# Down weights in runs of four rows, and gate and up products that take every fourth weight column

## The chip, the core and the metric

The kernel runs on one core of one Trainium2 chip. The metric is the device time of one execution, in microseconds (us); lower is better. The kernel before takes 1104.15 us, the median of 3 runs between 1103.52 and 1104.58. A core has a tensor engine (PE, with its weight loads shown apart as PEld), a vector engine (DVE), a scalar engine (ACT), a GpSimd engine (POOL), SyncE (SP), which here issues most transfers, and 16 DMA engines.

## The reference

One step of a one-layer encoder over 1104 tokens (64 sample tokens, 16 meta tokens and 1024 prompt tokens) with width 1024. A mixer comes first (projection, windowed pooling, gated linear attention, output projection, residual), then a mixture of experts: each token picks one of 4 groups and in it 2 of 8 experts, so 2 of 32. All in f32. The part that the change touches, cut to its core:

```python
D_EXPERT = D_MODEL // 2            # 512 hidden units for each expert
def expert_block(args):
    xb, e = args
    h = jax.nn.silu(xb @ w_eg[e]) * (xb @ w_eu[e])
    return h @ w_ed[e]
...
ys = lax.map(expert_block, (xs, block_e)).reshape(R, D)
ys = ys.astype(jnp.float32) * slot_gate[:, None]
out = jax.ops.segment_sum(ys, slot_tok, num_segments=T + 1)[:T]
```

`w_eg` and `w_eu` are 1024 x 512 for each expert, `w_ed` is 512 x 1024. The hidden units are summed over in the last product, so they may stand in any order, if it is the same in `h` and in the rows of `w_ed`.

## The kernel before

The tokens stand in 9 tiles of 128. A first stage, up to about 500 us, runs over the tiles: projections (`features`, L1178), attention, the output projection (L1303), the router, and the ranks of the tokens within their experts. Normalized rows go to a buffer in HBM, `hn_rows`. The copies that normalize them, L550 and L620 on ACT, read the 1024 numbers of a row in the order k, p from a layout p, k, so every eighth number is read; L555 is a copy with a scale that reads neighbouring numbers.

The expert stage runs over 32 experts, `expert(t, b)` with e = 2t + b, each with one block of 96 tokens. All is double-buffered by b. For one expert:

- GpSimd gathers 96 rows of `hn_rows`; TensorE turns them in eight pieces (`turn_rows`, L1166) and DVE writes them as `rowsT`, 128 x 8 x 96 (`xnT` or `hnT` in the trace).
- `up` (L1407 to L1414) forms the gate and then the up product. The hidden units go to the output's partitions: the weights are the operand that is loaded into the array, and the 96 token columns stream. Of the 512 units a block m takes 128, in two strips q of 64, which use the two halves of the array's columns side by side; k runs over eight parts of the width of 1024. That makes 4 x 8 x 2 = 64 products each for gate and up. The trace has two records, each with a weight load, for one such f32 product, so 256 of L1412 for an expert.
- ACT and DVE form `hid` = silu(gate) x up, 128 partitions (units) by 4 blocks of 96 tokens.
- `down` (L1423, L1429) sums over the units: `hid` is loaded as weights, and `wd[b][:, k, ...]` streams, k being the block of units.
- ACT copies the result out of PSUM and GpSimd scatters it to `pick_rows` in HBM.

The rows of the next expert are turned between `up` and `down`. The order on each engine is written out by hand, with semaphores between engines.

The weights come from HBM by SyncE's queue, 2 MB each: `load_weights(t, b)` issues gate (L394), up (L399) and down (L402). Each waits until its buffer of two experts ago is free: the gate buffer after `pe_g`, the up buffer after `pe_u2`, the down buffer after `pe_d`. In SBUF, gate and up lie as 128 partitions x 8 x 512: partition p holds eight neighbouring rows of the matrix, one run of 16 KB in HBM. Down lies as 128 x 4 x 1024: partition p holds the rows p, 128 + p, 256 + p and 384 + p, four runs of 4 KB. Unit 128m + p stands at partition p of block m, so `up` takes 64 neighbouring columns of its weights.

After the 32 experts a block for experts with over 96 tokens (L1472 on) would run; it uses the same functions and its own loads (L427 to L429). A last stage adds each token's two results and normalizes.

Of the kernel before, what the change touches and what calls it, by code (L numbers as in the profile page):

```python
# [28 lines left out]
P = 128  # L29
# [26 lines left out]
FF = D // 2  # L56
KF = FF // P
NL = GROUPS + NE
BLOCK = 96
# [58 lines left out]
def wait_parted(eng, sem, value, parted):  # L118


    eng.wait_ge(sem, value)
    if not isinstance(value, int):
        eng.sem_inc(parted, 1)
# [32 lines left out]
def build(nc, x_all, state_pool, state_gla, norm_mix, w_in, w_gate_up, b_gate, w_pool, pool_scale, gla_norm, w_out,  # L156
# [5 lines left out]
    with ExitStack() as ctx:  # L162
# [3 lines left out]
        def sem(name):  # L166
            return ctx.enter_context(nc.semaphore(name))
# [16 lines left out]
        wd = [arena[:, starts["d", b]:starts["d", b] + EW].rearrange("p (k n) -> p k n", k=KF) for b in range(2)]  # L184
# [140 lines left out]
        s = {n: sem(n) for n in names}  # L325
        g_in = [sem(f"g_in{b}") for b in range(2)]
        u_in = [sem(f"u_in{b}") for b in range(2)]
        d_in = [sem(f"d_in{b}") for b in range(2)]
# [18 lines left out]
        def _(sp):  # L347
# [44 lines left out]
            def load_weights(t, b):  # L392
                e = 2 * t + b
                sp.dma_start(wg[b], w_eg[bass.ds(e * D, D), :].rearrange("(p k) n -> p k n", k=KD)).then_inc(g_in[b], 16)  # L394
                if isinstance(t, int) and b == 1:
                    sp.wait_ge(s["pe_wout"], TILES)
                if not isinstance(t, int):
                    sp.wait_ge(s["pe_u2"], 2 * (e - 1))
                sp.dma_start(wu[b], w_eu[bass.ds(e * D, D), :].rearrange("(p k) n -> p k n", k=KD)).then_inc(u_in[b], 16)  # L399
                if not isinstance(t, int):  # L400
                    sp.wait_ge(s["pe_d"], e - 1)
                sp.dma_start(wd[b], w_ed[bass.ds(e * FF, FF), :].rearrange("(k p) n -> p k n", p=P)).then_inc(d_in[b], 16)  # L402

            sp.wait_ge(s["pe_v"], TILES)
            load_weights(0, 0)
            load_weights(0, 1)
            sp.wait_ge(s["sA_ready"], TILES)
            for p in range(PAIRS):
# [4 lines left out]
            with sp.Fori(1, NE // 2) as t:  # L413
                for b in range(2):

                    sp.wait_ge(s["pe_g"], 2 * t + b - 1)
                    load_weights(t, b)
# [5 lines left out]
            with sp.If(n_x > 0):  # L423
                with sp.Fori(0, EXTRA) as n:
                    with sp.If(n < n_x):
                        e = sp.value_load(steer[0:1, bass.ds(n + 1, 1)], min_val=0, max_val=NE - 1)
                        sp.dma_start(wg[0], w_eg[bass.ds(e * D, D), :].rearrange("(p k) n -> p k n", k=KD)).then_inc(s["x_w"], 16)  # L427
                        sp.dma_start(wu[0], w_eu[bass.ds(e * D, D), :].rearrange("(p k) n -> p k n", k=KD)).then_inc(s["x_w"], 16)
                        sp.dma_start(wd[0], w_ed[bass.ds(e * FF, FF), :].rearrange("(k p) n -> p k n", p=P)).then_inc(s["x_w"], 16)  # L429

                        wait_parted(sp, s["x_stored"], 16 * n + 16, s["parted"])
            sp.dma_start(g_fin, norm_final.partition_broadcast(P)).then_inc(s["g_fin_in"], 16)
# [729 lines left out]
        def _(pe):  # L1162
            mm = nc.tensor.matmul

            def turn(out, src, n):
                return nc.tensor.transpose(out, src, ident[0:n, 0:n])  # L1166
# [218 lines left out]
            for n in range(2):  # L1385
                for g in range(NG):
                    last = turn(bank[2 + n][0:HIST, g * P:(g + 1) * P], u_keep[:, n, g, :], P)
# [8 lines left out]
            SW = P // STRIPS  # L1396
# [10 lines left out]
            def up(out, w, b, blocks=range(KF)):  # L1407

                for n, m in enumerate(blocks):
                    for k in range(KD):  # L1410
                        for q in range(STRIPS):
                            last = mm(out[q * SW:(q + 1) * SW, n * BLOCK:(n + 1) * BLOCK], w[:, k, m * P + q * SW:m * P + (q + 1) * SW],  # L1412
                                      rowsT[b][:, k, :], start=k == 0, stop=k == KD - 1)
                return last  # L1414

# [24 lines left out]
            def expert(t, b, last=False):  # L1440
                e = 2 * t + b
                pe.wait_ge(s["eT_ready"], 2 * e + 2)
                pe.wait_ge(g_in[b], 16 * t + 16)
                up(bank[2 + b], wg[b], b).then_inc(s["pe_g"], 1)
                pe.wait_ge(u_in[b], 16 * t + 16)

                for half in range(2):
                    up(bank[4 + half], wu[b], b, HALVES[half]).then_inc(s["pe_u2"], 1)
                if not last:
                    turn_rows(e + 1, 1 - b, 16 * (t + b) + 16)  # L1450
                pe.wait_ge(d_in[b], 16 * t + 16)
                pe.wait_ge(s["hid_ready"], 2 * e + 2)
                if not (isinstance(t, int) and e == 0):
                    pe.wait_ge(s["ye_ready"], YE_STEPS * e)
                down(b).then_inc(s["pe_d"], 1)
# [21 lines left out]
            with pe.If(n_x > 0):  # L1477
                with pe.Fori(0, EXTRA) as n:
                    with pe.If(n < n_x):
                        pe.wait_ge(s["x_rows"], 16 * n + 16)  # L1480
                        for half in range(2):
                            for k in range(4):
                                c = (4 * half + k) * P
                                last = turn(bank[half][:, k * BLOCK:(k + 1) * BLOCK], rows[0][:, c:c + P], BLOCK)
                        last.then_inc(s["x_pe"], 1)
                        pe.wait_ge(s["x_w"], 48 * n + 48)
                        pe.wait_ge(s["x_dve"], X_STEPS * n + TILES + 2)
                        up(bank[2], wg[0], 0).then_inc(s["x_pe"], 1)
                        up(bank[4], wu[0], 0).then_inc(s["x_pe"], 1)
                        pe.wait_ge(s["x_dve"], X_STEPS * n + TILES + X_STEPS)  # L1490
                        down(0).then_inc(s["x_pe"], 1)
# [44 lines left out]
```

## Time and profile before

| | us |
|---|---|
| median of 3 runs | 1104.15 |
| the profiled execution | 1103.76 |
| its span, first to last instruction | 1101.9 |
| TensorE busy in the span | 1012.4 |
| VectorE busy | 417.4 |
| ScalarE busy | 240.8 |
| GpSimd busy | 104.8 |

Mean granted clock of TensorE over the span: 0.966. The profile has a page of sums and a trace that can be asked for details. Busy times are sums of records; in the profile the ends of matmuls are modelled, and matmuls are pipelined, so a busy TensorE says that it has work, not that it is at its peak. Where one engine waits for another, the trace gives the idle time and the line that ended it. "issue" there is a wait that the profile explains by nothing it shows.

### The profile page before, as it was taken

To read this page: it belongs to the slowest core of one execution; us is meant where nothing else is said; L and a number is where in the kernel's file an instruction comes from. 1 tells how busy PE (TensorE), PEld (TensorE's weight loads), DVE (VectorE), ACT (ScalarE), POOL (GpSimd) and SP (SyncE) were. 2 spreads that over 40 slices of the span, in tenths; PEclk is the share of its full clock that TensorE was granted. 3 is DMA by queue.
4 is the path that set the end of the run, shared out by engine and by line. 5 is a ranking of instruction groups with operands and counts; after the bars stand their busy time and mean duration, and the time that the engine had idled before them with its cause. 6 is when DMAs were issued, how large, how long until landed. Compare 5 with 4: busy or idle time off the path is not lost.

```text
span 1101.9 us, 32850 instructions
## 1 busy us (share of the span) xinstructions
PE 1012.4 (92%) x14634; PEld 822.7 (75%) x14634; DVE 417.4 (38%) x909; ACT 240.8 (22%) x506; POOL 104.8 (10%) x172
## 2 busy tenths in 40 slices
PE   5999999999999999875999999999999999999920
PEld 5786777768685958435888898898888888988910
DVE  1434443535253535243432332332322323323338
ACT  2352232323332321210111111011111111111123
POOL 0110101010110101001111011011110110110000
PEclk9999999999999999986999999999999999999965
DMA  8900000000000000384999999999999999999557
GB/s 272 402 5 39 1 39 0 38 0 38 4 34 38 0 38 1 152 322 173 373 375 393 405 399 411 408 404 401 398 410 403 395 409 404 397 405 401 215 214 300
DMA packets 50850, 262.17 MB, mean 238 GB/s; under 512 B 8205, under 2 KB 10701, under 8 KB 42618
## 3 DMA queue, kind: packets, MB, share of 16 engines
q1 hardware_dynamic: 41050, 234.05, 53.8%
q0 software_dynamic: 7168, 18.10, 4.8%
q10 hardware_dynamic: 2592, 9.44, 2.1%
q8 instruction: 31, 0.51, 0.2%
q14 instruction: 9, 0.07, 0.0%
HBM read 241.84 MB, written 26.80 MB: 244 GB/s over the span
## 4 chain that ended last, share of the span: by engine, by line
PE 91%; DVE 5%; DMA 2%; issue 1%; ACT 1%; SPq 0%; ACTq 0%; DVEq 0%; POOLq 0%; POOL 0%
PE bank L1412 31%; PE bank L1178 18%; PE bank L1303 11%; PE bank L1423 10%; PE bank L1230 6%; PE bank L1429 5%; PE bank L1166 4%; DVE arena L1144 1%; DVE arena L1142 1%; PE bank L1279 1%; DMA arena<-in_w_in 1%; DVE arena L1150 1%; PE bank L1237 1%; PE bank L1296 1%; PE bank L1290 1%
## 5 line engine op out<-in xcount | busy, mean ns | idle before, releaser
L1178 PE MATMUL bank<-xnT,arena 128*128 128x128 f32 x1728 | 201.5, 278 | 4.9 <-DMA arena<-in_w_in 3.5
L1178 PEld LDWEIGHTS bank<-xnT,arena 128*128 128x128 f32 x1728 | 197.1, 193 | 7.6 <-DMA arena<-in_w_in 4.0
L1412 PEld LDWEIGHTS bank<-xnT,arena 128*64 128x64 f32 x4096 | 171.8, 138 | 8.9 <-issue 8.9
L1412 PE MATMUL bank<-xnT,arena 128*64 128x96 f32 x4096 | 175.0, 248 | 2.2 <-issue 2.2
L1412 PEld LDWEIGHTS bank<-hnT,arena 128*64 128x64 f32 x4096 | 169.6, 137 | 7.4 <-issue 7.4
L1412 PE MATMUL bank<-hnT,arena 128*64 128x96 f32 x4096 | 172.8, 246 | 0.6 <-issue 0.6
L1026 DVE TENSOR_SCALAR mixT<-mixT 128x384 f32<-128x384 f32 x32 | 11.5, 360 | 324.0 <-ACT mixT L692 324.0
L1303 PE MATMUL bank<-arena,mixT 128*128 128x512 f32 x288 | 127.8, 602 | 3.0 <-DVE mixT L859 3.0
L1303 PEld LDWEIGHTS bank<-arena,mixT 128*128 128x128 f32 x288 | 54.9, 193 | 69.4 <-issue 65.7
L1423 PE MATMUL bank<-arena,silu_r 128*32 128x384 f32 x768 | 86.0, 487 | 0.5 <-issue 0.5
L1429 PE MATMUL bank<-arena,silu_r 128*32 128x256 f32 x384 | 85.9, 380 | 0.0
L1429 PE MATMUL bank<-arena,osq 128*32 128x256 f32 x384 | 85.9, 380 | 0.0
L1423 PE MATMUL bank<-arena,osq 128*32 128x384 f32 x768 | 85.8, 488 | 0.0
L1027 DVE RECIPROCAL mixT<-mixT 128x384 f32<-128x384 f32 x32 | 81.7, 2553 | 1.1
L1230 PE MATMUL bank<-arena,xnT 128*128 128x512 f32 x144 | 64.6, 592 | 0.0
L1429 PEld LDWEIGHTS bank<-arena,osq 128*32 128x32 f32 x384 | 40.9, 110 | 15.0
L697 ACT ACTIVATE hs<-bank 96x384 f32<-96x384 f32 x32 | 13.8, 482 | 174.3 <-PE bank L1429 174.3
L697 ACT ACTIVATE kz_v<-bank 96x384 f32<-96x384 f32 x32 | 13.8, 482 | 173.5 <-PE bank L1429 173.5
L1429 PEld LDWEIGHTS bank<-arena,silu_r 128*32 128x32 f32 x384 | 40.9, 110 | 14.4
L460 POOL TENSOR_TENSOR window_work<-window_work 128x568 f32<-128x568 f32 x9 | 10.2, 1132 | 401.4 <-ACT window_work L586 401.4
L1230 PEld LDWEIGHTS bank<-arena,xnT 128*128 128x128 f32 x144 | 26.1, 190 | 26.3 <-issue 26.3
L692 ACT ACTIVATE mixT<-bank 128x384 f32<-128x384 f32 x32 | 15.7, 490 | 127.0 <-PE bank L1412 127.0
(193 smaller groups left out, 934.8 us busy)
## 6 DMA issues: line engine op xcount, KB each, us to landing
arena<-in_w_eg SPq DMA_DIRECT2D x32, 2048.0 KB
arena<-in_w_eu SPq DMA_DIRECT2D x32, 2048.0 KB
arena<-in_w_ed SPq DMA_DIRECT2D x32, 2048.0 KB, 15.4
hn_rows<-hs ACTq DMA_DIRECT2D x18, 512.0 KB, 3.5
arena<-pick_rows SPq DMA_DIRECT2D x16, 512.0 KB, 10.1
arena<-in_w_in SPq DMA_DIRECT2D x3, 2048.0 KB, 14.5
arena<-in_w_out SPq DMA_DIRECT2D x1, 4096.0 KB, 25.7
out_y_prompt<-arena SPq DMA_DIRECT2D x8, 512.0 KB, 3.5
```

The lines of the kernel that those rows point to most:

```text
L692: A(sig[:, 0:NH], bank[2 + b][:, 0:NH], ACT.Exp, scale=-1.0).then_inc(s["sig_ready"], 1)
L697: A(ye[b][:, half * OWN:(half + 1) * OWN], bank[6 + half][0:BLOCK, 0:OWN], ACT.Copy).then_inc(s["ye_ready"], 1)
L1026: moe.then(V.tensor_scalar(gs[:, 0:NH], sig[:, 0:NH], 1.0, None, ALU.add))
L1027: moe.then(V.reciprocal(gs[:, 0:NH], gs[:, 0:NH]))
L1142: final.then(V.scalar_tensor_tensor(out=y1[i][0:r, :], in0=y1[i][0:r, :], scalar=gate_all[0:r, i, 0:1], in1=h_all[0:r, i, :], op0=ALU.mult ...
L1166: return nc.tensor.transpose(out, src, ident[0:n, 0:n])
L1178: last = mm(out, w_in_sb[:, k, a:b], xnT[:, k, :], start=k == 0, stop=k == KD - 1)
L1230: last = mm(bank[6][:, :], xnT[:, k, :], w_in_sb[:, k, V0:R0], start=k == 0, stop=k == KD - 1)
L1303: done = mm(bank[n][:, :], mixT[:, k, :], w_out_sb[:, k, n * 512:(n + 1) * 512], start=k == 0, stop=k == KD - 1)
L1412: last = mm(out[q * SW:(q + 1) * SW, n * BLOCK:(n + 1) * BLOCK], w[:, k, m * P + q * SW:m * P + (q + 1) * SW], rowsT[b][:, k, :], start=k ...
L1423: last = mm(bank[6 + half][g * TG:(g + 1) * TG, 0:OWN], tokens(k, g), wd[b][:, k, half * OWN:(half + 1) * OWN], start=k == 0, stop=k == KF ...
L1429: return mm(bank[n][TGS * TG:P, c:c + REST], tokens(k, g), wd[b][:, k, 2 * OWN:D], start=k == 0 and c == 0, stop=k == KF - 1, skip_group_c ...
```

## The change

The down weights are loaded with four neighbouring rows to a partition, so that partition p holds rows 4p to 4p + 3 (one run of 16 KB). Partition p of block m in `wd` is then unit 4p + m, and `up` has to put unit 4p + m there as well: for strip q it takes the 64 columns from 4 x 64 q + m on, every fourth. The columns of one load then lie 16 bytes apart. In the list of instructions of the built kernel nothing moves on any engine, and no wait and no shape of a product changes; the down load's destination is written as 128 x 4096 in place of 128 x 4 x 1024.

```diff
@@ load_weights, on SyncE
-                sp.dma_start(wd[b], w_ed[bass.ds(e * FF, FF), :].rearrange("(k p) n -> p k n", p=P)).then_inc(d_in[b], 16)
+                sp.dma_start(wd[b], w_ed[bass.ds(e * FF, FF), :].rearrange("(p k) n -> p k n", k=KF)).then_inc(d_in[b], 16)
@@ the block for experts with over 96 tokens, on SyncE
-                        sp.dma_start(wd[0], w_ed[bass.ds(e * FF, FF), :].rearrange("(k p) n -> p k n", p=P)).then_inc(s["x_w"], 16)
+                        sp.dma_start(wd[0], w_ed[bass.ds(e * FF, FF), :].rearrange("(p k) n -> p k n", k=KF)).then_inc(s["x_w"], 16)
@@ up, on TensorE
                 for n, m in enumerate(blocks):
                     for k in range(KD):
                         for q in range(STRIPS):
-                            last = mm(out[q * SW:(q + 1) * SW, n * BLOCK:(n + 1) * BLOCK], w[:, k, m * P + q * SW:m * P + (q + 1) * SW],
+
+                            units = slice(KF * q * SW + m, KF * (q + 1) * SW, KF)
+                            last = mm(out[q * SW:(q + 1) * SW, n * BLOCK:(n + 1) * BLOCK], w[:, k, units],
                                       rowsT[b][:, k, :], start=k == 0, stop=k == KD - 1)
```

P = 128, KD = 8, KF = 4, SW = 64, BLOCK = 96, FF = 512.

## Rows read from the trace of the kernel before

**Rows 1.** The page: span, and busy time by engine.
```profile
span 1101.9 us, 32850 instructions
PE 1012.4 (92%) x14634; PEld 822.7 (75%) x14634; DVE 417.4 (38%) x909; ACT 240.8 (22%) x506; POOL 104.8 (10%) x172
```
**Rows 2.** The page: chain that ended last, shares by engine and by line.
```profile
PE 91%; DVE 5%; DMA 2%; issue 1%; ACT 1%; SPq 0%; ACTq 0%; DVEq 0%; POOLq 0%; POOL 0%
PE bank L1412 31%; PE bank L1178 18%; PE bank L1303 11%; PE bank L1423 10%; PE bank L1230 6%; PE bank L1429 5%; PE bank L1166 4%; DVE arena L1144 1%; DVE arena L1142 1%; PE bank L1279 1%; DMA arena<-in_w_in 1%; DVE arena L1150 1%; PE bank L1237 1%; PE bank L1296 1%; PE bank L1290 1%
```
**Rows 3.** Groups of L1412: operands, shapes, count | busy us, mean ns | idle before.
```profile
L1412 PE MATMUL bank<-xnT,arena 128*64 128x96 f32 x4096 | 175.0, 248 | 2.2 <-issue 2.2
L1412 PE MATMUL bank<-hnT,arena 128*64 128x96 f32 x4096 | 172.8, 246 | 0.6 <-issue 0.6
L1412 PEld LDWEIGHTS bank<-hnT,arena 128*64 128x64 f32 x4096 | 169.6, 137 | 7.4 <-issue 7.4
```
**Rows 4.** A stretch of 30 us in the expert stage, with its header.
```profile
core 0: us, PE busy (x) PEld busy (x) DVE busy (x) ACT busy (x) POOL busy (x), PEclk, DMA share, GB/s
890.00:920.00 30.00, 30.00 (x590) 25.78 (x586) 10.41 (x14) 4.45 (x11) 3.40 (x6) 1.00 1.02 400
```
**Rows 5.** The chain from 581 us: start, us, what. One expert and the next.
```profile
581.65 10.71 PE bank L1412 x256
592.37 0.81 PE bank L1166 x8
...
598.49 10.71 PE bank L1412 x256
```
**Rows 6.** Down loads (L402): 600 to 640 us, then landing at 960 to 1000.
```profile
L402 SPq DMA_DIRECT2D arena<-in_w_ed x2: 384/384/384, 615.5 to 632.4; - x2
DMA to landing us min/median/max: 14.8/14.9/15.0
DMA to landing us min/median/max: 17.6/17.8/18.0
```
**Rows 7.** Issue of gate and of down loads: ns min/median/max, first and last start.
```profile
L394 SPq DMA_DIRECT2D arena<-in_w_eg x32: 332/333/1192, 459.2 to 1008.3; - x32
L402 SPq DMA_DIRECT2D arena<-in_w_ed x32: 383/384/436, 460.0 to 1019.7; - x32
```
**Rows 8.** Waits: who <- for whom: us in total, times, longest.
```profile
SPq L402 <- PE bank L1429: 173.6, 30, 6.0
PE bank L1412 <- issue: 2.8, 3, 1.2
```
**Rows 9.** Loads from 800.48 us, at 0.02 and at 0.08 us: start, us.
```profile
800.49 0.14 PEld L1412 LDWEIGHTS bank<-hnT,arena 128*64 128x64 f32 x2 [0.41 <-issue]
800.49 0.20 PEld L1412 LDWEIGHTS bank<-hnT,arena 128*64 128x64 f32 x4 [0.41 <-issue]
```
**Rows 10.** Matmuls of L1412 with hnT: ns min/median/max.
```profile
L1412 PE MATMUL bank<-hnT,arena x4096: 246/246/298, 528.6 to 1046.8; 128*64 128x96 f32 x196
```
**Rows 11.** Turns of 15 x 128: loads by the timeline, and ns of one.
```profile
32.20 0.32 PEld L1166 LDWEIGHTS bank<-cst,osq 15*128 15x128 f32 x4
L1166 PEld LDWEIGHTS bank<-cst,osq x4: 136/138/138, 32.2 to 32.4; 15*128 15x128 f32 x4
```
**Rows 12.** Groups of ScalarE: copies of 128 x 1024 with a scale.
```profile
L555 ACT ACTIVATE arena<-arena,mix_scale 128x1024 f32<-128x1024 f32 x8 | 8.6, 1137 | 0.0
L620 ACT ACTIVATE hs<-h_all,hss 128x1024 f32 x6 | 12.9, 2150 | 0.7
L620 ACT ACTIVATE hs<-h_all,hss 128x1024 f32<-128x1024 f32 x3 | 6.4, 2145 | 0.1
```
**Rows 13.** Groups of L1178: 128 weight columns, 128 rows streamed.
```profile
L1178 PE MATMUL bank<-xnT,arena 128*128 128x128 f32 x1728 | 201.5, 278 | 4.9 <-DMA arena<-in_w_in 3.5
L1178 PEld LDWEIGHTS bank<-xnT,arena 128*128 128x128 f32 x1728 | 197.1, 193 | 7.6 <-DMA arena<-in_w_in 4.0
```
**Rows 14.** Router product: loads of 32 columns, by the timeline.
```profile
460.80 0.66 PEld L1321 LDWEIGHTS bank<-w_r_sb,hnT 128*32 128x32 f32 x64 [0.17 <-issue]
```

## Prediction

> **What bounds the kernel now.** I read the page first, by engine [rows 1]: TensorE is busy for 1012.4 of 1101.9 us. A busy TensorE need not be the bound, so the chain that ended last comes next [rows 2]: 91% of it is TensorE, and its largest line is L1412, the gate and up products that the change rewrites, with 31%, some 342 us. The groups [rows 3] show what these are: 4096 + 4096 matmul records, each with its weight load, 64 weight columns against 96 rows of tokens. A stretch of the expert stage [rows 4], one of fourteen like it, then tells whether anything else holds it: TensorE is busy in all of the 30 us, at a granted clock of 1.00 (the level of 2.4 GHz). The DMA engines are at 1.02 of a full share too, so they are a candidate. The chain through two experts [rows 5] settles it: 256 records of L1412 in 10.71 us, turns, down products, and the next expert's L1412 begins 16.84 us after the last (598.49 - 581.65), with no other engine and no transfer between. The transfers keep up with little to spare: a down load lands 14.9 us after its issue at 600 to 640 us and 17.8 us at 960 to 1000 [rows 6]. So the queue falls back, by some 2.9 us over 21 experts, 0.14 us per expert. Its slack: the load issued at 615.5 us [rows 6] belongs to the expert after the next, so it is wanted 16.84 us and then 11.5 us of L1412 and turns later [rows 5], 28 us in all, and is there after 15 to 18. Over 10 us of slack remain at the end of the stage.
>
> A record in L1412 costs 10.71 us / 256 = 41.8 ns. Two strips of 64 columns stand beside each other in the array, so one strip has 83.7 ns for a record, and 32 experts have 32 x 128 = 4096 such periods. That number, 4096, carries the sum: each ns of the period is 4.1 us.
>
> **The down load.** The edit in the load loop turns 512 runs of 4 KB into 128 runs of 16 KB, for the same 2 MB. The nearest row is the gate load, which already has runs of 16 KB: its issue takes 0.33 us of SyncE's queue, that of the down load 0.38 [rows 7]. That 0.05 us is hidden: SyncE's queue waits for TensorE between the loads, 173.6 us before the down loads alone [rows 8]. The packets themselves may go faster; from above, the queue's lag of 0.14 us per expert goes, and from below nothing changes. In both cases no transfer stands in the chain [rows 5], so I take 0. If the cover were gone, the full change would be worth what the lag is, 0.14 x 32 = 4.5 us. There is one place where a transfer may touch TensorE: in the first experts it stands still inside L1412 without a semaphore, 2.8 us in three waits [rows 8]. If these are late instruction fetches behind the weights, larger runs may shorten or lengthen them, by -2.8 to +2.8 us. I take 0. The same load in the block for overflowing experts costs nothing: there are exactly 8192 = 32 x 256 records of L1412 [rows 3], so the block was never entered.
>
> **The arithmetic.** The same products are formed, since partition p of block m now holds hidden unit 4p + m in both operands. The number of instructions, their order, waits and shapes stay. Nothing is moved past a queue and no wait is added. What is left is how long a weight load takes when its 64 columns lie 16 bytes apart, and not side by side.
>
> **What a load costs now.** At the start of an expert's L1412 nothing is in flight in the array. The first two loads (one for each strip) end 0.14 us after the start, and with the next two it is 0.20 us [rows 9]: the second pair began some 0.06 us after the first. Over the whole line a matmul takes 246 ns at the median and 298 at the most [rows 10]; the matmuls of that first pair are such long ones, and the 52 ns more are their wait for the load. So a load of 64 columns occupies its strip for about 55 ns. It is hidden, since the 96 rows stream for 83.7 ns meanwhile: 28.7 ns of cover. The load is hidden as long as it takes under 83.7 / 55 = 1.52 of its present time, 1.31 ns per column.
>
> **What a spread load costs.** No matmul or load of this trace reads columns apart, so I bound it.
> - From below: 15 x 128 turns have almost nothing to stream, and four of their loads of 128 columns, each 138 ns, fit into 0.32 us [rows 11]. So one follows another after (0.32 - 0.138) / 3 = 0.061 us, 0.48 ns per column. The read path can deliver twice as fast as L1412's loads ask of it (55 / 64 = 0.86 ns). If spreading halves that best rate, a load takes 0.95 x 64 = 61 ns, still under 83.7, and the price is 0.
> - From above: ScalarE shows what a spread read costs. L555 and L620 are both a copy of 128 x 1024 with a scale from memory; L555 reads side by side and takes 1137 ns, L620 reads every eighth column and takes 2150 and 2145 [rows 12]. That is a factor of 1.89, or 0.99 ns more per element, or 2.1 ns for each. By these the load of 64 columns takes 1.89 x 55 = 104, or 55 + 63 = 118, or 64 x 2.1 = 134 ns. All three are above 83.7. Below nothing is excluded: a spread load has no way to end sooner that I can see, and by itself it would gain nothing.
>
> The ScalarE rows are the only ones of a spread read, so I take the value by them, rounded to a doubling: 2 x 55 = 110 ns. What a period is when the load takes that long has a row: L1178's loads have 128 side-by-side columns (2 x 55 = 110) against 128 rows, and a record there takes 201.5 / 1728 = 116.6 ns [rows 13]. So the period becomes 110 to 116.6 ns; I take 113.5. That is 29.8 ns more per period, 4096 x 29.8 = 122 us, or 3.8 us in each expert. The ends: 104 ns gives 20.3 x 4096 = 83 us, 118 with the same 3.5 ns of handing over 121.5, so 155 us, and 134 gives 50.3 x 4096 = 206 us.
>
> The Trainium skill has a rule on this. After the row on ScalarE: "Advanced Engine Details and Errata", section "SBUF Cachelines", says that the memory is read in lines of 16 bytes, that two hits on a line are needed to hide its latency, and that a different line at every access is penalised. Four f32 columns are just 16 bytes, so every read would hit a new line, and the load would lengthen; the ScalarE rows agree with it at a spread of 32 bytes. The Trainium skill's page "SBUF — State Buffer", section "Door 1: The DMA port swizzle", adds to the same rule that four f32 are how far one can stride for free. By that reading the load stays at 55 ns and the sum is 0. No row here is at just 16 bytes, so the trace can't decide between the two.
>
> **Sum.** The profiled execution took 1103.76 us, of which 1101.9 are the span; the median of the runs is 1104.15, 0.4 above it. 1103.76 + 122 = 1226 us. Experts then take 20.6 us, the transfers still some 17.0 (16.84 and the lag), and so the DMA share of the stage falls to 0.82. That relief is worth nothing, for TensorE is later.
>
> **Rivals.**
> - The spread load stays hidden: 1104 us, 1103 to 1105. For it: 28.7 ns of cover, and a read path that serves 128 columns in 61 ns. Against it: the only spread reads in the trace take nearly twice as long, and a factor of 1.52 is enough to come out of cover.
> - Faster: the load is hidden and the larger runs let instruction fetches through in the first experts. It takes away at most the 2.8 us of waits [rows 8], so some 1101 to 1103. Against it: the gate and up loads, two thirds of the bytes, have runs of 16 KB already, and no wait there is shown to be a transfer's.
> - Slower by far: the two strips' loads, which now overlap, take turns when they are spread, 2 x 110 = 220 ns per period, 136 x 4096 = 558 us more, 1662 us. Against it: four loads of 32 columns side by side follow each other so fast in the router product, 64 in 0.66 us [rows 14], that they must overlap, and I know no reason why spreading should end that.
>
> **How the numbers follow.** What a measurement of this kernel tells from no change is about 0.2%, 2.2 us. My forecast, a load between 104 and 134 ns, has 0.55: 1187 to 1310 us by its own range, 1226 as its value. A load that lengthens to just about the cover (80 to 100 ns, 5 to 80 us more) is in between, with 0.04. The hidden load has 0.30, faster 0.06, and loads in turn 0.05. So slower is 0.55 + 0.04 + 0.05 = 0.64, same 0.30, faster 0.06. For 8 times in 10 the range must take in the hidden load, since without it 0.4 would be left out; it goes from 1102 to 1315. What is left out is loads in turn, most of the faster case, and some of the error in the main case.
>
> **What would show it.** Right: L1412's 256 records take 14 to 15 us in the chain, its load records grow from 137 ns to some 190, matmuls keep 246 ns or grow by the wait, an expert takes 20.6 us, the DMA share falls and the down load's landing time goes below 14 us. Line L1303 and everything ahead of 500 us, as the down products, stay as they are. Wrong: L1412 stays at 10.71 us per expert though its load records are longer (then the cover was enough), or nothing changes in them at all (then a spread of 16 bytes is free). Stretches of L1412 above 20 us would mean that loads no longer overlap.

## The result and the profile after

The changed kernel takes 1255.18 us (median of 4 runs, 1254.23 to 1255.44), the kernel before in the same comparison 1103.84 (1102.75 to 1104.58). The ratio is 1.137, with an interval of 1.1351 to 1.139: 151 us slower.

The page of the changed kernel: span, busy time by engine, and the shares of the chain that ended last.

```profile
span 1252.3 us, 32850 instructions
PE 1164.6 (93%) x14634; PEld 975.7 (78%) x14634; DVE 417.7 (33%) x909; ACT 240.8 (19%) x506; POOL 103.9 (8%) x172
...
PE bank L1414 40%; PE bank L1178 16%; PE bank L1303 10%; PE bank L1425 9%; PE bank L1230 5%; PE bank L1431 5%; PE bank L1166 3%; DVE arena L1144 1%; DVE arena L1142 1%; PE bank L1279 1%; DMA arena<-in_w_in 1%; DVE arena L1150 1%; PE bank L1237 1%; PE bank L1296 1%; PE bank L1290 0%
...
L1414 PEld LDWEIGHTS bank<-hnT,arena 128*64 128x64 f32 x4096 | 247.0, 217 | 6.6 <-issue 6.6
L1414 PE MATMUL bank<-xnT,arena 128*64 128x96 f32 x4096 | 250.7, 285 | 1.2 <-issue 1.2
L1414 PE MATMUL bank<-hnT,arena 128*64 128x96 f32 x4096 | 249.6, 284 | 0.0
L1178 PE MATMUL bank<-xnT,arena 128*128 128x128 f32 x1728 | 201.4, 278 | 5.0 <-DMA arena<-in_w_in 3.6
```

L1414 is what was L1412 (and L1425 and L1431 are L1423 and L1429, the down products). Its matmuls have a busy time of 250.7 + 249.6 = 500.3 us, against 175.0 + 172.8 = 347.8 in [rows 3]: 152.5 us more. The span grew by 150.4. L1178 has 201.4 us against 201.5 [rows 13]. So the whole loss is in the rewritten products; the other lines together give back some 2 us.

The chain of the changed kernel through one expert, and the same stretch of 30 us as [rows 4]:

```profile
618.88 15.53 PE bank L1414 x256
634.41 0.81 PE bank L1166 x8
640.53 15.54 PE bank L1414 x256
```
```profile
890.00:920.00 30.00, 30.00 (x466) 26.72 (x466) 7.75 (x13) 2.48 (x6) 2.33 (x4) 1.00 0.85 313
```

An expert takes 640.53 - 618.88 = 21.65 us instead of 16.84, and L1414 15.53 instead of 10.71 [rows 5]. A strip's period grew from 83.7 to 15.53 / 128 = 121.3 ns, and 37.6 ns x 4096 = 154 us. TensorE has work in all of the stretch at the same granted clock, and the page's busy shares of 93% and 92% hardly tell the two kernels apart. What tells is that fewer records fit into 30 us (466 against 590), and that a load record grew from 137 to 217 ns. The DMA share fell from 1.02 to 0.85.

The loads at the start of an expert's L1414, two views that end 0.24 us apart; then all records of the line (ns min/median/max):

```profile
618.81 0.32 PEld L1414 LDWEIGHTS bank<-hnT,arena 128*64 128x64 f32 x4 [0.41 <-issue]
618.81 0.44 PEld L1414 LDWEIGHTS bank<-hnT,arena 128*64 128x64 f32 x6 [0.41 <-issue]
```
```profile
L1414 PEld LDWEIGHTS bank<-hnT,arena x4096: 192/217/217, 532.2 to 1197.2; 128*64 128x64 f32 x196
L1414 PE MATMUL bank<-hnT,arena x4096: 282/283/357, 532.2 to 1197.3; 128*64 128x96 f32 x196
```

The third pair of loads ends 0.12 us after the second, so the new period is there from the start of the line. The matmul's median grew from 246 ns [rows 10] to 283, by the 37 ns that it waits for its weights.

The down load's issue and landing in the changed kernel (600 to 700 us, then over the whole run):

```profile
L402 SPq DMA_DIRECT2D arena<-in_w_ed x4: 333/333/333, 619.1 to 684.0; - x4
DMA to landing us min/median/max: 7.9/8.3/17.9
```

It is issued in 0.33 us and lands after some 8 us at the median in place of 15 to 18 [rows 6]: with TensorE late, the queue has time.

### The profile page after: what moved, and what is told of

It reads as the page before. It is cut to its first block, busy times and chain, and to the rows that moved or that the text cites. A ratio compares the mean times of both kernels' runs of the same rounds, so it can differ in the third digit from the quotient of the medians.

```text
span 1252.3 us, 32850 instructions
## 1 busy us (share of the span) xinstructions
PE 1164.6 (93%) x14634; PEld 975.7 (78%) x14634; DVE 417.7 (33%) x909; ACT 240.8 (19%) x506; POOL 103.9 (8%) x172
## 4 chain that ended last, share of the span: by engine, by line
PE 92%; DVE 4%; DMA 2%; issue 1%; ACT 1%; SPq 0%; ACTq 0%; DVEq 0%; POOLq 0%; POOL 0%
PE bank L1414 40%; PE bank L1178 16%; PE bank L1303 10%; PE bank L1425 9%; PE bank L1230 5%; PE bank L1431 5%; PE bank L1166 3%; DVE arena L1144 1%; DVE arena L1142 1%; PE bank L1279 1%; DMA arena<-in_w_in 1%; DVE arena L1150 1%; PE bank L1237 1%; PE bank L1296 1%; PE bank L1290 0%
## 5 line engine op out<-in xcount | busy, mean ns | idle before, releaser
L1414 PEld LDWEIGHTS bank<-xnT,arena 128*64 128x64 f32 x4096 | 248.1, 217 | 7.6 <-issue 7.6
L1414 PEld LDWEIGHTS bank<-hnT,arena 128*64 128x64 f32 x4096 | 247.0, 217 | 6.6 <-issue 6.6
L1414 PE MATMUL bank<-xnT,arena 128*64 128x96 f32 x4096 | 250.7, 285 | 1.2 <-issue 1.2
L1414 PE MATMUL bank<-hnT,arena 128*64 128x96 f32 x4096 | 249.6, 284 | 0.0
L1178 PE MATMUL bank<-xnT,arena 128*128 128x128 f32 x1728 | 201.4, 278 | 5.0 <-DMA arena<-in_w_in 3.6
L1178 PEld LDWEIGHTS bank<-xnT,arena 128*128 128x128 f32 x1728 | 197.1, 193 | 7.6 <-DMA arena<-in_w_in 4.0
L1425 PE MATMUL bank<-arena,silu_r 128*32 128x384 f32 x768 | 85.8, 487 | 0.5 <-issue 0.5
L1431 PE MATMUL bank<-arena,osq 128*32 128x256 f32 x384 | 85.9, 380 | 0.0
L1431 PE MATMUL bank<-arena,silu_r 128*32 128x256 f32 x384 | 85.9, 380 | 0.0
L1425 PE MATMUL bank<-arena,osq 128*32 128x384 f32 x768 | 85.8, 488 | 0.0
L1431 PEld LDWEIGHTS bank<-arena,silu_r 128*32 128x32 f32 x384 | 40.9, 110 | 15.0
L1431 PEld LDWEIGHTS bank<-arena,osq 128*32 128x32 f32 x384 | 40.9, 110 | 15.0
```

The source lines that it names most:

```text
L1178: last = mm(out, w_in_sb[:, k, a:b], xnT[:, k, :], start=k == 0, stop=k == KD - 1)
L1425: last = mm(bank[6 + half][g * TG:(g + 1) * TG, 0:OWN], tokens(k, g), wd[b][:, k, half * OWN:(half + 1) * OWN], start=k == 0, stop=k == KF ...
L1431: return mm(bank[n][TGS * TG:P, c:c + REST], tokens(k, g), wd[b][:, k, 2 * OWN:D], start=k == 0 and c == 0, stop=k == KF - 1, skip_group_c ...
```

## The experiments

All runs are one change from the kernel before or from the changed one, but for e10, which has two. Where only a part of the change is made, or another step is taken, the units of `hid` no longer match the rows of the down weights, as the expectation says; the times are read as times of the same work. The chain is read between 800 and 880 us where nothing else is said.

**The down load alone (e1).**

```diff
-                sp.dma_start(wd[b], w_ed[...].rearrange("(k p) n -> p k n", p=P))
+                sp.dma_start(wd[b], w_ed[...].rearrange("(p k) n -> p k n", k=KF))
```

> The down load with four rows to a partition alone; gate and up products take neighbouring columns as before, so the units of hid and of the down weights don't match in this run. Theory L (a spread weight load outlasts the stream of 96 rows; the transfers are not in the chain): 1102 to 1105 us, the same as before, L1412 at 10.71 us for 256 records, the down load's landing time no longer growing. Rival D (the new transfers themselves hurt, by writes of 16 KB into one partition while TensorE reads): 1200 us or more, L1412 above 12 us. Rival G (a hidden gain of the larger runs): 1098 to 1101 us.

1104.38 us (before 1102.82), ratio 1.0012, interval 0.9999 to 1.0025. One row of its chain, and the down load's landing at 600 to 640 and at 960 to 1000 us:

```profile
800.88 10.71 PE bank L1412 x256
```
```profile
DMA to landing us min/median/max: 13.7/14.2/14.7
DMA to landing us min/median/max: 19.9/20.3/20.6
```

The transfers neither cost nor gain. D and G are out. But my detail was wrong: the landing time still grows, and by more than before, 6.1 us in place of 2.9. The larger runs did not stop the queue from falling back. (Each of these stretches has two down loads of one execution, so the amount is rough.)

**The columns alone (e2).**

```diff
-                            last = mm(out[...], w[:, k, m * P + q * SW:m * P + (q + 1) * SW],
+                            units = slice(KF * q * SW + m, KF * (q + 1) * SW, KF)
+                            last = mm(out[...], w[:, k, units],
```

> Gate and up products take every fourth column, the down load is that of before, so the units don't match in this run. Theory L: 1255 us within 2, L1414 at 15.5 us for 256 records, a period of 120 ns. Rival D (the transfers share in the cost): clearly less than 1250, at the most 1200 us.

1254.16 us, ratio 1.1372 (1.1349 to 1.1396): the whole loss, with the down load as it was before. Its chain:

```profile
836.43 15.53 PE bank L1414 x256
```

**Other steps: two, three and eight columns (e3, e12, e4).** e3 is a full version of the idea with runs of two rows:

```diff
-                            units = slice(KF * q * SW + m, KF * (q + 1) * SW, KF)
+                            units = slice(2 * P * (m // 2) + 2 * q * SW + m % 2, 2 * P * (m // 2) + 2 * (q + 1) * SW, 2)
...
+                sp.dma_start(wd[b].rearrange("p (m r) n -> p m r n", r=2), w_ed[...].rearrange("(m p r) n -> p m r n", p=P, r=2))
```

> Two neighbouring down rows to a run (8 KB), and every second column in the gate and up products: columns 8 bytes apart, two on each line of 16 bytes. Theory L in its form that a line read costs one fixed time of some 1.9 ns: 64 columns are 32 lines, 60 ns, which the stream hides: 1102 to 1106 us, L1414 at 10.7 us. Rival W (any load that isn't of neighbouring columns takes the long way, whatever its step): as after, 1255 us. Rival P (the price grows with the step): about 1150 us.

e12, from the changed kernel:

```diff
-                            units = slice(KF * q * SW + m, KF * (q + 1) * SW, KF)
+                            first = 40 * (STRIPS * m + q)
+                            units = slice(first, first + 3 * SW, 3)
```

> Gate and up products take every third column (12 bytes apart; the units don't match the down weights, so the result is not the reference's). 64 columns then touch 48 lines of 16 bytes, against 32 at a step of two and 64 at a step of four. Theory F (each line costs 1.87 ns): 90 ns for a load, just over the stream: a period of 90 to 92 ns, L1415 at 11.5 to 11.8 us, 27 to 34 us more, about 1135 us. Rival C (only a step of a whole line is slow, less is free): 1103 us, the same as before. Rival P (two hits on a line are needed, so any line with one hit pays in full): about 1200 us.

e4, from the changed kernel:

```diff
-                            units = slice(KF * q * SW + m, KF * (q + 1) * SW, KF)
+                            units = slice(STRIPS * m + q, FF, FF // SW)
```

> Every eighth column (32 bytes apart), the down load as in the changed kernel, so the units don't match in this run. Theory L (one line for each column already at a step of four, so a wider step costs no more): 1255 us within 5. Rival P (the price grows with the step): 1400 us or more, a period of 180 ns or more.

The chain of each, in this order (in e12 three of 256 records are missing from the trace; its turns are 17.43 us apart):

```profile
816.51 10.71 PE bank L1414 x256
```
```profile
820.95 0.81 PE bank L1166 x8
827.08 11.30 PE bank L1415 x253
838.38 0.81 PE bank L1166 x8
```
```profile
816.85 15.62 PE bank L1414 x256
```

| step | lines of 16 bytes for 64 columns | period, ns | time, us | ratio (interval) |
|---|---|---|---|---|
| 1 (before) | 16 | 83.7 | | 1 |
| 2 (e3) | 32 | 83.7 | 1103.70 | 1.0009 (0.9996 to 1.0021) |
| 3 (e12) | 48 | 11.30 / 128 = 88.3 | 1121.88 | 1.0159 (1.0142 to 1.0176) |
| 4 (after) | 64 | 121.3 | 1255.18 | 1.137 (1.1351 to 1.139) |
| 8 (e4) | 64 | 15.62 / 128 = 122.0 | 1259.23 | 1.1419 (1.1395 to 1.1443) |

Doubling the step from four to eight adds 0.7 ns to the period, so the price does not follow the distance. It follows the lines of 16 bytes touched: 121.3 / 64 = 1.9 ns and 88.3 / 48 = 1.8 ns for each line, and at a step of two 32 x 1.9 = 61 ns, which the stream hides. W, P and, by e12, C are out. e12 came out somewhat below what I expected of F: a period of 88.3 and not 90 to 92, so 4.6 ns x 4096 = 19 us more and not 27 to 34; measured are 17.0 (1121.88 against 1104.88 for the kernel before in the same comparison). So close to the cover, a small error in the load is a large one in the price.

The load records tell more, for they show the load also where the stream hides it. Steps one, two, three and eight (ns min/median/max; step four, above, has 192/217/217):

```profile
L1412 PEld LDWEIGHTS bank<-hnT,arena x4096: 132/137/137, 528.6 to 1046.7; 128*64 128x64 f32 x196
L1414 PEld LDWEIGHTS bank<-hnT,arena x4096: 136/138/140, 528.3 to 1045.9; 128*64 128x64 f32 x196
L1415 PEld LDWEIGHTS bank<-hnT,arena x4096: 164/169/178, 530.1 to 1064.6; 128*64 128x64 f32 x196
L1414 PEld LDWEIGHTS bank<-hnT,arena x4096: 194/218/225, 533.5 to 1202.6; 128*64 128x64 f32 x196
```

At a step of two the load is not only hidden, it is hardly longer: 138 ns against 137. A fixed price for each line can't be the whole of it either, since 16 lines of neighbours would then cost 16 x 1.9 = 30 ns, and e6 below has 60.8. What fits all five steps, read after the runs and not forecast, is a count of columns that are alone on their line: none at steps one and two, 32 at a step of three (the other 32 lie in pairs on 16 lines), 64 at four and eight. The shortest records grow from 132 ns by 4, 32, 60 and 62, so by 0.94 to 1.0 ns for each column that is alone, on top of the 60.8 / 64 = 0.95 ns that each column costs anyway.

**Is it the load's own time, or does something beside it stretch it? (e5, e6, e9)** Fewer rows stream, so the load is laid bare. e5, from the changed kernel (e6 is the same edit from the kernel before, e9 has ROWS = 8):

```diff
+            ROWS = 48
...
-                            last = mm(out[q * SW:(q + 1) * SW, n * BLOCK:(n + 1) * BLOCK], w[:, k, units],
-                                      rowsT[b][:, k, :], start=k == 0, stop=k == KD - 1)
+                            last = mm(out[q * SW:(q + 1) * SW, n * BLOCK:n * BLOCK + ROWS], w[:, k, units],
+                                      rowsT[b][:, k, 0:ROWS], start=k == 0, stop=k == KD - 1)
```

> The changed kernel, but gate and up products stream 48 of the 96 rows (the other half of hid is left as it lies, so the result is not the reference's). The stream then takes some 40 ns of a period. Theory A (a spread load of 64 columns takes some 117 to 120 ns by itself, whatever streams): the period stays at 117 to 120 ns, L1414 at 15.0 to 15.5 us for 256 records, about 1245 to 1255 us. Rival S (alone it takes 97 ns, and the streams take read time from it): 100 to 108 ns, 12.8 to 13.8 us, about 1170 to 1200 us.

1252.57 us, ratio 1.1353 (1.1302 to 1.1404). Its chain:

```profile
811.20 15.49 PE bank L1415 x256
```

Half the stream and the same period, 15.49 / 128 = 121.0 ns: the load sets it. Theory A holds.

> The kernel before with 48 of the 96 rows streamed in the gate and up products. It gives the time of a load of neighbouring columns, which the stream hides in the kernel before. If the 55 ns read at the start of the line hold, the period is 55 to 60 ns, L1412 at 7.0 to 7.7 us, and 1104 - 32 x 3.3 = some 1000 us, if the transfers allowed it; they need some 16.9 us for an expert, so theory A and rival S both expect 1100 us or a little less, with TensorE waiting for weights.

1102.19 us, ratio 0.9994 (0.9982 to 1.0007). Its chain from 578 us, where gate and up products stand apart, and its waits on transfers (us in total, times, longest):

```profile
578.42 3.89 PE bank L1413 x128
```
```profile
PE bank L1424 <- DMA arena<-in_w_ed: 40.2, 22, 2.8
PE bank L1413 <- DMA arena<-in_w_eu: 14.6, 15, 1.4
PE bank L1413 <- DMA arena<-in_w_eg: 9.6, 9, 1.4
```

The period is 3.89 / 64 = 60.8 ns. Half the stream would ask for some 42 (half of 83.7, an estimate), so I take 60.8 as the load of neighbours; no run with a still shorter stream confirms it. The cover in the kernel before was real, then: the load took some 55 to 61 ns of 83.7. Twice 60.8 is 121.6, the period of the changed kernel within 0.3 ns. The total did not fall by the 32 x 3 us that TensorE saved, since 64.4 us (the three rows together) went into waits for weights. The kernel before stands just at the limit of its transfers too.

> The changed kernel with 8 of 96 rows streamed in the gate and up products (most of hid is left as it lies, so the result is not the reference's). With 48 rows the period of a strip stayed at 121 ns. Theory A (120 ns is the load's own time, and where the first load of an expert seems to take 95 to 97 ns that is only how a run begins): the period stays at 117 to 121 ns, about 1250 us. Rival S (the load alone takes 95 to 97 ns and any stream beside it stretches it): with the stream down to some 7 ns of a period it falls to 95 to 105 ns, about 1155 to 1190 us.

1323.52 us, ratio 1.1983 (1.1959 to 1.2007). The total is over 70 us above theory A's 1250 and further from rival S's, while the period is theory A's. Its chain, and its stretch that covers L1415 of that expert (columns as in [rows 4]):

```profile
819.21 15.46 PE bank L1415 x256
834.68 1.47 PE bank L1166 x8
```
```profile
819.30:834.60 15.30, 15.30 (x256) 15.28 (x256) 3.83 (x4) 2.49 (x6) 2.33 (x4) 0.60 0.84 308
```

The matmuls have 8 columns to stream now, not 96, and the granted clock is 0.60 in the mean of this stretch, so mostly at the lower level of 1.2 GHz, where it was 1.00 in the kernel before. Turns take 1.47 us for eight, against 0.81 [rows 5], and what follows up to the next expert's L1415 6.95 us (843.10 - 836.15), against 5.31 in the changed kernel (640.53 - 635.22). An expert takes 23.89 us in place of 21.65, and 32 x 2.24 = 72 us. The spread loads do not notice: 15.46 / 128 = 120.8 ns at this clock, 121.3 at 1.00.

**One strip at a time (e7, e8).** e7 from the changed kernel, e8 the same from the kernel before:

```diff
-                    for k in range(KD):
-                        for q in range(STRIPS):
+                    for q in range(STRIPS):
+                        for k in range(KD):
```

> The changed kernel with the products of strip 0 first, then those of strip 1, so that only one strip loads and streams at a time. The result is that of the changed kernel. Theory A: 120 ns for each of 256 records, 30.7 us, 15.2 us more in an expert, about 1740 us. Rival S2 (the other strip's loads and stream lengthen the load, which alone takes 97 to 107 ns): 25 to 27.5 us, about 1560 to 1640 us.

> The kernel before with the strips in turn: one stream at a time. Both theories: the load of 55 ns stays hidden, 82 to 84 ns for each of 256 records, 21.2 us in place of 10.7, about 1440 us. It is the zero for the run of the changed kernel with strips in turn.

e7 1554.38 us, ratio 1.4089; e8 1308.10 us, ratio 1.1857. By the total e7 looks like S2: 24.89 us for 256 records, 97 ns each. The first loads say otherwise. A strip has 16 records before the other's turn comes; these are the first ten loads, the first 13 and the first 19, and then the chain:

```profile
821.82 1.27 PEld L1414 LDWEIGHTS bank<-xnT,arena 128*64 128x64 f32 x10 [0.41 <-issue]
821.82 1.63 PEld L1414 LDWEIGHTS bank<-xnT,arena 128*64 128x64 f32 x13 [0.41 <-issue]
821.82 1.99 PEld L1414 LDWEIGHTS bank<-xnT,arena 128*64 128x64 f32 x19 [0.41 <-issue]
```
```profile
821.89 24.89 PE bank L1414 x256
```

A record of a load is 217 ns, so ten loads follow each other at (1.27 - 0.217) / 9 = 0.117 us. Inside one strip's run the loads keep the period of 117 to 120 ns without a neighbour; the mean of 97 comes from the borders, where the next strip's loads start before this one's are done: loads 14 to 19 add 1.99 - 1.63 = 0.36 us, 0.06 for each, the pace at which two strips load together in the changed kernel (121.3 / 2 = 60.7 ns). The zero run shows the same: e8 has 17.17 us where 256 x 83 ns would be 21.2, so it too was not fully one at a time, and both theories' number of 1440 us was wrong. S2 is out, and so is my rival that the two strips' loads take turns.

```profile
814.86 17.17 PE bank L1412 x256
```

**Turns with spread loads (e11).** From the kernel before:

```diff
-                        c = (4 * half + k) * P
-                        last = turn(bank[half][:, k * BLOCK:(k + 1) * BLOCK], rows[b][:, c:c + P], BLOCK)
+                        c = 4 * half + k
+                        last = turn(bank[half][:, k * BLOCK:(k + 1) * BLOCK], rows[b][:, c:D:KD], BLOCK)
```

> The kernel before, but the turns of the gathered rows load every eighth of their columns (32 bytes apart) and not 128 neighbours, so the width is in another order than the weights' and the result is not the reference's. A turn takes 101 ns now, and its load of neighbouring columns at best 61. Theory F (each spread column takes a fixed time of the read path, 120 / 64 = 1.87 ns): 240 ns for a turn, 1.9 us for eight in place of 0.81, 35 us in all, about 1139 us. Rival M (a spread load takes twice the time of the same load of neighbours): 122 ns, 1.0 us for eight, 5 us in all, about 1109 us.

1110.19 us, ratio 1.0053 (1.0035 to 1.0071). Its turns in the chain, and their loads:

```profile
814.25 1.06 PE bank L1166 x8
```
```profile
814.18 0.97 PEld L1166 LDWEIGHTS bank<-cst,window_work 96*128 96x128 f32 x8
```

Eight turns take 1.06 us, not 0.81; 1.9 was theory F's, and 1.0 with some 1109 us rival M's, which held. Their loads follow each other at about (0.97 - 0.207) / 7 = 0.109 us (a record is 207 ns) for 128 columns on 128 lines: 0.85 ns per line, not 1.9. So F as I had put it falls. In both cases a spread load is about twice that of neighbours: 109 ns for the turn against 61 for the turns of 15 rows [rows 11], a factor of 1.8, and 121 against 61 for the product. It would fit if a product's f32 load read each column twice and a turn's once, with 0.85 to 0.94 ns for each line read. That is an argument from two numbers, and no run shows it.

**What the larger runs are worth where transfers bind (e10).** e6 with the down load of e1.

> Neighbouring columns and 48 of 96 rows streamed, as in the run that made the transfers the bound (1102.2 us, a ratio of 0.9994 to the kernel before), but with the down load in runs of 16 KB. It gives the worth of the new load where transfers are the bound. If larger runs move faster (32 packets of 4 KB to 8 of 16 KB for each DMA engine): 1094 to 1100 us. If they don't (the down load alone let the queue fall back faster than before): 1102 to 1112 us.

1092.95 us, ratio 0.9886 (0.9867 to 0.9906), against 0.9994 (0.9982 to 1.0007) for e6: 9 us (0.8%) by the medians, 1.1% or 12 us by the ratios, which are the fairer measure since e6 ran in another comparison. It is just below the expected range. Its waits on transfers sum to 55.9 us, against 64.4:

```profile
PE bank L1413 <- DMA arena<-in_w_eg: 24.4, 19, 1.7
PE bank L1424 <- DMA arena<-in_w_ed: 19.3, 21, 1.4
PE bank L1413 <- DMA arena<-in_w_eu: 12.2, 21, 0.7
```

So with the runs of 16 KB the kernel is faster there. How much of it is the transfers' and how much the clock's (0.952 for e6 and 0.959 for e10 over their spans) is open, and so is why the landing time grew faster in e1.

## Why the prediction held, and what was off

- **The bound.** TensorE's L1412 was named from the chain, with transfers close behind. e6 confirms both: without 3 us of L1412 per expert, the transfers hold the kernel at 1102 us.
- **The mechanism.** A spread load comes out from under the stream. e2 has the whole loss with the old transfers, e5 shows that the load sets the period.
- **The size of the load: the term that was off.** I took a doubling of 55 ns, 110, and with 3.5 ns of handing over a period of 113.5. Measured are 121.3: 37.6 ns more, not 29.8, 152.5 us and not 122. By e6 the doubling was right and the base was low. The 55 ns came from the first loads of a line, by ends that the view gives to 0.01 us, and the row on L1178, by which I priced the handing over, was for a load and a stream of one length. In steady work, with the stream halved, a load of neighbours has a period of 60.8 ns (e6), and twice that is 121.6.
- **The signs.** L1414 took 15.53 us (said: 14 to 15), load records 217 ns (190), an expert 21.65 us (20.6), the DMA share 0.85 (0.82), and the down load landed after 8.3 us (below 14). All went the way that was said, most of them further.
- **The ScalarE rows.** The factor of 1.89 gave 104 ns, too little, and 2.1 ns for each column 134, too much. 0.99 ns more for each element gave 118 and, with the handing over, a period of 121.5, almost what was measured; for another engine and a load of another base that is a coincidence as far as the runs go. For the turn's load it would be 61 + 128 x 0.99 = 188 ns, and e11 has 109.
- **From below.** I took the best rate from the turns, 0.48 ns per column, and let it take twice as long: 0.95. For a turn that is near what e11 shows, 0.85. It does not carry over to the products' loads, which pay 1.9. The bound was from a load of another kind.
- **The rule with two readings.** The change decides it for this load: four f32 apart is not free here, and two apart is (e3). The Trainium skill's "Advanced Engine Details and Errata", section "SBUF Cachelines", with its two hits on a line, agrees with all five steps. At a step of three it holds line by line: of e12's 64 columns the 32 that are alone on a line are slow (32 ns more in the shortest load record), and the 32 that lie in pairs are not. Four apart is a step at which every column is alone.
- **The transfers.** Worth 0, as e1 shows (ratio 1.0012). The upper bound, that the queue's lag goes, had the wrong sign in e1's trace, where the lag grew.
- **The first experts.** Waits of L1414 without a cause in the profile went from 2.8 us [rows 8] to 1.2 us, within the 2.8 allowed, and no part of the answer.
- **Rivals.** The hidden load is out by 151 us, faster by its sign, and loads in turn by e7. With 0.30 on the hidden load the forecast was open on the main question, and the range of 1102 to 1315 us took in both answers; the value of 1226 us is 29 below the measured 1255.

## What to carry to other kernels

A weight load that the profile never shows as a wait can still be close to its cover: compare the load's own time (from the first, uncovered load of a burst, or from a run with a shorter stream) with the period before touching its layout. In these f32 products the operand that is loaded into the array may be read with a step of two at next to no cost; with three a load takes some 88 ns in place of 61, and with four or eight twice as long. If a layout has to give way for a transfer, check first that the transfer is in the chain: here it was worth nothing, and what it asked of TensorE cost 14%.

## What the runs showed of the hardware beyond that

- The spread load's time did not change with TensorE's clock: 120.8 ns per period at a mean granted clock of 0.60 (e9), 121.3 at 1.00.
- A step of three columns costs in between: a period of 88.3 ns. The price follows the columns that are alone on a line of 16 bytes, about 1 ns for each in these products.
- Streaming 8 columns for each load, and not 96, took the granted clock from 1.00 to 0.60 in that stretch, and the kernel from 1255 to 1324 us although it did less.
